# Differential attention beside a recurrent mixer: position term and softmax factors as TensorE products, and each head's output split into four parts

## The reference, cut to what matters

```python
def diff_attention(q, k, v, lam, slopes):      # q, k: 4 heads, 2 maps each of 64 channels; v: 128 channels a head
    ...
    dist = (qpos[:, None] - kpos[None, :])
    s = jnp.einsum('bhcqd,bhckd->bhcqk', qblk, kh) * scale
    s = s - slopes[None, :, None, None, None] * dist
    s = jnp.where(dist >= 0, s, NEG_INF)
    pr = jax.nn.softmax(s, axis=-1)
    attn = pr[:, :, 0] - lam * pr[:, :, 1]
    return jnp.einsum('bhqk,bhkv->bhqv', attn, vh)
```

## Time and profile before

| | |
|---|---|
| median of 3 runs | 1692.66 us (1690.74 to 1696.22) |
| the profiled execution: its own time | 1689.58 us |
| the profiled execution: span | 1687.8 us |
| TensorE busy | 1525.4 us (90% of the span) |
| VectorE busy | 1093.8 us (65%) |
| ScalarE busy | 705.6 us (42%) |
| mean granted clock of TensorE | 0.957 of full speed |

### The profile page before, as it was taken

The page is one execution under the profiler, slowest core; times in us unless marked ns, Lnnn a source line. Parts: engine busy times, 40 slices in busy tenths (PEclk is TensorE's granted clock), DMA queues, the critical chain, the costliest instruction groups (busy, mean ns, idle before and its releaser), DMA issues.

```text
span 1687.8 us, 26133 instructions
## 1 busy us (share of the span) xinstructions
PE 1525.4 (90%) x10702; PEld 1272.3 (75%) x10702; DVE 1093.8 (65%) x1661; ACT 705.6 (42%) x1057; POOL 58.9 (3%) x52
## 2 busy tenths in 40 slices
PE   5999888988989999999989989999999888778892
PEld 4889666866768888888868778787799666777882
DVE  5831766676479737737679997454765446567775
ACT  5422434433444333333444222334344346357773
POOL 0000000000000000000000000000000000222221
PEclk9999889998989999999989999999999999689996
DMA  6220000002412222222312222232243203569896
GB/s 245 100 100 1 2 2 3 3 2 75 151 53 97 101 100 100 100 89 90 122 50 100 100 75 100 77 135 88 88 150 128 72 26 122 192 222 364 322 329 219
DMA packets 37828, 189.69 MB, mean 112 GB/s; under 512 B 4304, under 2 KB 4432, under 8 KB 24400
## 3 DMA queue, kind: packets, MB, share of 16 engines
q1 hardware_dynamic: 30672, 167.08, 28.2%
q0 software_dynamic: 4864, 16.78, 2.7%
q10 hardware_dynamic: 2176, 4.19, 0.7%
HBM read 175.46 MB, written 12.58 MB: 111 GB/s over the span
## 4 chain that ended last, share of the span: by engine, by line
PE 70%; DVE 17%; DMA 6%; ACT 4%; issue 3%; POOL 0%; DVEq 0%; SPq 0%; POOLq 0%; ACTq 0%
PE acc L470 18%; PE acc L472 18%; PE acc L471 18%; DMA raw<-wstream 4%; DVE CA L2382 3%; PE acc L712 2%; DVE wl L1915 2%; PE mb L712 1%; PE mb L614 1%; DVE wl L1903 1%; PE mb L545 1%; PE acc L1015 1%; ACT wh L1230 1%; PE mb L470 1%; PE mb L472 1%
## 5 line engine op out<-in xcount | busy, mean ns | idle before, releaser
L470 PE MATMUL acc<-XH,wh 128*128 128x512 f32 x1008 | 397.3, 394 | 5.9 <-DVE wl L1915 4.9
L472 PE MATMUL acc<-XH,wl 128*128 128x512 f32 x1008 | 393.1, 390 | 0.0
L471 PE MATMUL acc<-XL,wh 128*128 128x512 f32 x1008 | 392.8, 390 | 0.0
L1230 ACT ACTIVATE wh<-raw 128x2048 fp32r<-128x2048 f32 x99 | 189.4, 1915 | 248.2 <-DMA raw<-wstream 248.2
L1915 DVE TENSOR_TENSOR wl<-raw,wh 128x2048 fp32r<-128x2048 f32 x99 | 226.0, 2287 | 71.7 <-ACT wh L1230 68.5
L470 PEld LDWEIGHTS acc<-XH,wh 128*128 128x128 f32 x1008 | 189.7, 188 | 48.1 <-DVE wl L1915 5.8
L471 PEld LDWEIGHTS acc<-XL,wh 128*128 128x128 f32 x1008 | 189.7, 188 | 41.1 <-issue 2.2
L472 PEld LDWEIGHTS acc<-XH,wl 128*128 128x128 f32 x1008 | 189.5, 188 | 39.9
L1251 ACT ACTIVATE ev<-acc 128x512 f32<-128x512 f32 x146 | 85.7, 598 | 217.8 <-PE acc L472 197.1
L1903 DVE TENSOR_TENSOR wl<-raw,wh 128x1024 fp32r<-128x1024 f32 x96 | 117.0, 1223 | 47.2 <-ACT wh L1217 40.9
L1217 ACT ACTIVATE wh<-raw 128x1024 fp32r<-128x1024 f32 x96 | 101.4, 1060 | 35.9 <-DMA raw<-wstream 35.3
(11 more groups left out here) (524 smaller groups left out, 2739.9 us busy)
## 6 DMA issues: line engine op xcount, KB each, us to landing
raw<-wstream SPq DMA_DIRECT2D x99, 1024.0 KB
raw<-wstream SPq DMA_DIRECT2D x96, 512.0 KB
YG<-YT ACTq DMA_DIRECT2D x8, 512.0 KB
XT<-xT SPq DMA_DIRECT2D x2, 1024.0 KB, 9.6
XT<-xT SPq DMA_DIRECT2D x1, 2048.0 KB, 7.8
XD<-HN SPq DMA_DIRECT2D x4, 512.0 KB, 2.6
out<-XTK SPq DMA_DIRECT2D x4, 512.0 KB, 2.6
cst<-consts SPq DMA_DIRECT2D x1, 1230.0 KB, 18.3
```

The costliest lines, as they stand in the source:

```text
L470: mm(out_, a[0], b[0], start=start, stop=False)
L471: mm(out_, a[0], b[1], start=False, stop=False)
L472: return mm(out_, a[1], b[0], start=False, stop=stop)
L1230: actv(wh[:, n % RING].rearrange("p a b c -> p (a b c)"), raw[:, n % RING, :], ACT.Copy).then_inc(hi_done, 1)
```

## The change

The distance table is copied once to float32r (`far`), and a 128x128 diagonal matrix holds the head's slope (`slopes`). `scores` adds, behind the product of each map, a float32r product of `slopes` with `far` over the same w columns, into the same bank. VectorE's `att_scaled` is gone; the maximum (`att_max`) and `exp` read the scores in PSUM. `exp` of a head's first unit waits for the maxima of its first two units.

`att_weights` no longer passes over `SC`: it writes two diagonal matrices `inv` with 1/den and lam/den. `turn` takes a float32 product of each block of each map with them, two for each block where one transpose stood; they add up in PSUM.

The output of heads 0 to 2 is issued in parts: the first product at `s6`, the second at `s7`, the third and fourth in the next pair's `nr`, behind its first products. The head's square, sums and root move to the next pair's `ak`, and `head_spread` to the end of `ak`. Head 3 keeps its old places.

Some names move to other beats: `max1` into level 2 before the level's last VectorE step, `scores2`'s maximum to the end of level 5, `turn2` between the two halves of `gh`, `exps` ahead of `exp3`, the table load behind `exp3`, `hats` to `s4`, `hat_r` ahead of `weights3`, and `weights3` to `s5` just before `turn3`.

```diff
-SIDE = {"l1": ["scores0", "scores1"], "l2": ["max1"], "l3": ["weights1"], "l4": ["scores2"], "x": ["weights2"],
-        "wu": ["turn2", "turned2"], "s2": ["up", "max3"], "s3": ["decay", "up_gate", "exp3", "exps"],
-        "s4": ["weights3", "scaled"], "s5": ["turn3", "turned3", "hats", "hat_r"], "s6": ["out", "square", "hat"],
-        "s7": ["sums", "more"], "y": ["root"], "mu": ["ends"]}
+SIDE = {"l1": ["scores0", "scores1"], "l3": ["weights1"], "l4": ["scores2"], "x": ["weights2"],
+        "wu": ["turned2"], "s2": ["up", "max3"], "s3": ["decay", "up_gate", "exps", "exp3", "root_table"],
+        "s4": ["scaled", "hats"], "s5": ["hat_r", "weights3", "turn3", "turned3"], "s6": ["out", "square", "hat"],
+        "s7": ["out_2nd", "sums", "more"], "y": ["root"], "mu": ["ends"]}
...
 scores(u)
                 for c in range(2):
-                    last = mm(score_of(u, c), QT[64 * c:64 * c + 64, h, i * P:(i + 1) * P],
-                              KD[64 * c:64 * c + 64, h, 0:w], start=True, stop=True)
+                    mm(score_of(u, c), QT[64 * c:64 * c + 64, h, i * P:(i + 1) * P],
+                       KD[64 * c:64 * c + 64, h, 0:w], start=True, stop=False)
+                    last = mm(score_of(u, c), slopes[:, :], far[:, S - w:S], start=False, stop=True)
...
 turn(u)
                 for j in range(u % TT + 1):
-                    last = nc.tensor.transpose(turned_of(u)[:, j * P:(j + 1) * P], SC[:, u % 2, 0, j * P:(j + 1) * P], ident)
+                    for c in range(2):
+                        last = mm(turned_of(u)[:, j * P:(j + 1) * P], SC[:, u % 2, c, j * P:(j + 1) * P],
+                                  inv[:, u % 2, c, :], start=(c == 0), stop=(c == 1))
...
-            def head_out(h):
+            def out_part(h, js):
                 pe.wait_ge(s["at_te"], TT * (h + 1))
-                for j in range(TT):
+                for j in js:
...
+            def head_out(h):
+                out_part(h, (0,) if h < 3 else range(TT))
+            def head_out_2nd(h):
+                if h < 3:
+                    out_part(h, (1,))
...
 nr(ct), behind its first products
                 if ct:
-                    head_spread(ct - 1)
+                    out_part(ct - 1, (2, 3))
 ak(ct)
                 if ct:
                     mu(ct - 1)
+                    head_sums(ct - 1)
...
                     products(hh, 1, KH).then_inc(s["rk_ak"], 1)
+                if ct:
+                    head_spread(ct - 1)
 gh(ct)
                     last.then_inc(s["rk_gh"], 1)
+                    if hh == 0:
+                        turn(TT * ct + 2)
...
 exp(u)
-                act.wait_ge(s["at_mx"], u + 1)
+                act.wait_ge(s["at_mx"], u + 1 + (u % TT == 0))
+                if u >= 2:
+                    act.wait_ge(s["at_t"], u - 1)
...
-                    last = actv(SC[:, u % 2, c, 0:w], SC[:, u % 2, c, 0:w], ACT.Exp, bias=nmx[:, x:x + 1],
+                    last = actv(SC[:, u % 2, c, 0:w], score_of(u, c), ACT.Exp, bias=nmx[:, x:x + 1],
...
 before_mu(ct) on ScalarE
                 if ct:
+                    head_square(ct - 1)
                     mu(ct - 1)
+                    head_root(ct - 1)
...
 att_weights(u)
-                link(v.tensor_scalar(a, a, rden[:, x:x + 1], None, ALU.mult))
-                v.scalar_tensor_tensor(out=a, in0=b, scalar=rden[:, x + 1:x + 2], in1=a, op0=ALU.mult,
-                                       op1=ALU.add).then_inc(s["at_p"], 1)
+                for c in range(2):
+                    last = v.tensor_scalar(inv[:, u % 2, c, :], ident, rden[:, x + c:x + c + 1], None, ALU.mult)
+                last.then_inc(s["at_p"], 1)
...
 head_norm(h)
+                if h < 3:
+                    slopes_of(h + 1)
...
 ak(ct) on VectorE
                     masked(AKRK, hh, 1)
+                if ct:
+                    head_root(ct - 1)
 level(l) on VectorE
                     if l == 2:
                         key_root(ct + 1)
                         att_max(TT * ct)
-                    if l == 5:
-                        att_scaled(TT * ct + 2)
+                        att_max(TT * ct + 1)
...
                     if l == 5:
-                        att_top(TT * ct + 2)
+                        att_max(TT * ct + 2)
...
+            v.tensor_copy(far[:, :], cs("alibi"))
+            slopes_of(0)
             dve.wait_ge(acc_ready, 20)
```

More of the change, by code:

```diff
@@ L187, in build @@
         Fo = at("Fo", [KT, S], ar + 32 * KB)
+        far = at("far", [S], top_of["cst"] + 4 * CO["alibi"][0], F32R)
+        slopes = at("slopes", [P], ar + 56 * KB, F32R)
+        inv = at("inv", [2, 2, P], ar + 56 * KB + 512)
         HH = at("HH", [KT, S], ar, F32R)
@@ L875, in _ @@
             main |= {f"l{l}": level(l) for l in range(1, LEVELS)} | {f"s{c}": enter(c) for c in range(2, NCH)}
-            in_beats(main, {"scores": scores, "turn": turn, "head_out": head_out, "head_sums": head_sums,
+            in_beats(main, {"scores": scores, "turn": turn, "head_out": head_out, "head_out_2nd": head_out_2nd, "head_sums": last_sums,
                             "up": up, "up_gate": up_gate})
@@ L1470, in affine, with root_table, last_square, last_root @@
                      scale=pr("ln_x_w", ct)).then_inc(s["rk_sd"], 1)
+            def root_table(ct):
+                actv(sml[:, 60:61], cs("eps", 0, 1), ACT.Sqrt)
+            def last_square(h):
+                if h == 3:
+                    head_square(h)
+            def last_root(h):
+                if h == 3:
+                    head_root(h)
             def before_mu(ct):
@@ L1969, in _, with att_max, slopes_of @@
             lowered[0] = B0["out"] + 3
-            def att_scaled(u):
-                h, i = divmod(u, TT)
-                w = (i + 1) * P
-                slope = 2.0 ** (-8.0 * (h + 1) / 4)
+            def att_max(u):
+                i = u % TT
+                w, first = (i + 1) * P, P * (i == 1)
                 dve.wait_ge(s["at_sc"], u + 1 + (i == 0))
                 if u >= 2:
-                    dve.wait_ge(s["at_t"], u - 1)
-                for c in range(2):
-                    link(v.scalar_tensor_tensor(out=SC[:, u % 2, c, 0:w], in0=cs("alibi", S - w, S), scalar=slope,
-                                                in1=score_of(u, c), op0=ALU.mult, op1=ALU.add))
-            def att_top(u):
-                w = (u % TT + 1) * P
+                    dve.wait_ge(s["at_e"], u - 1)
                 x = slice(2 * (u % 2), 2 * (u % 2) + 2)
-                link(v.tensor_reduce(mx[:, x], SC[:, u % 2, :, 0:w], AX.X, ALU.max))
+                link(v.tensor_reduce(mx[:, x], mb[:, 2:4, first:first + w], AX.X, ALU.max))
                 v.tensor_scalar(nmx[:, x], mx[:, x], -1.0, None, ALU.mult).then_inc(s["at_mx"], 1)
-            def att_max(u):
-                att_scaled(u)
-                att_top(u)
+            def slopes_of(h):
+                return v.tensor_scalar(slopes[:, :], ident, 2.0 ** (-8.0 * (h + 1) / 4), None, ALU.mult)
             def att_weights(u):
-                w, x = (u % TT + 1) * P, 2 * (u % 2)
-                a, b = SC[:, u % 2, 0, 0:w], SC[:, u % 2, 1, 0:w]
+                x = 2 * (u % 2)
                 dve.wait_ge(s["at_e"], u + 1)
@@ L2251, in _ @@
             main |= {f"l{l}": level(l) for l in range(1, LEVELS)} | {f"s{c}": enter(c) for c in range(2, NCH)}
-            in_beats(main, {"max": att_max, "weights": att_weights, "head_root": head_root,
-                            "decay": decay, "hat_r": hat_r, "scaled": scaled, "hats": hats, "hat": hat, "ends": last_in, "more": more_in})
+            in_beats(main, {"max": att_max, "weights": att_weights, "head_root": last_root, "decay": decay, "hat_r": hat_r, "scaled": scaled, "hats": hats, "hat": hat, "ends": last_in, "more": more_in})
             dve.wait_ge(s["rk_vs"], 7)
```

12 lines of the change are left out of this document (8 added, 4 removed).

## The result

The changed kernel takes 1742.8 us (median of four runs, 1738.0 to 1749.0) against 1691.7 for the kernel before beside it: a ratio of 1.030, 95% interval 1.026 to 1.034. It is 51 us slower. The forecast had the sign, but 20 of the 51 us, and its range ended at 1720. The profiled execution took 1749.0 us, with a span of 1747.2; it is the longest of the four, while the one of the kernel before (1689.6) is short among its own.

A forecast was written before the change was run, and what follows sets the result against it. TensorE bounds a round's front, a chain of hand-overs its tail. Front of round 0 2.35, rounds 1 to 3 13.05, tails 2.4, round 3's tail 2.8: +20.6 on 1689.6, plus 1.8, gives 1712 us; range 1688 to 1720.

The forecast's parts named there:

- step 1: Whole stage: VectorE loses some 15 us of L1979 and some 6 of the weights, costed at nothing in a round's front.
- step 2: Scores: the position product parts the two maps' products, +0.8, +0.8 and +1.1 us by unit, +2.7 a round.
- step 4: Start of rounds 1 to 3: `head_spread` waits for the reciprocal behind VectorE's second mask, level 1 starts +2.0 us later.
- step 3: Turns as products: units 0 and 1 +0.75, unit 2 1.45, unit 3 1.9 us at full clock, 3.5 at half.
- Step 5: Tail of rounds 0 to 2: unit 3's turn late behind `hat_r`, at half clock, `y` +0.8 us, bounds -1.1 and +2.1.
- Rival A: Scores: the position product slips between the maps' products without parting them, 1.55 us a round less, 1706; chance 0.14.
- the forecast's first lines: Tail of a round: L614, square and sums ahead of `y`, 6.3 us a round, are what can come off the path.
- Step 6: Round 3's tail: splits ahead of `weights3` delay unit 3's turn, output ends 2.8 us later; bounds +0.9 and +4.6.
- Rival C: Tails: half the clock lasts longer, +2.1 us in rounds 0 to 2 and +4.6 in the last, 1718; chance 0.10.
- Rival B: Tails: the clock holds at 2.4 GHz, -1.1 us in rounds 0 to 2 and +0.9 in the last, 1704; chance 0.12.

The follow-up runs named there:

- experiment 16: Changed kernel with only ScalarE's and VectorE's lists behind the third state put back in their old order: 1.0160 of the kernel before.
- experiment 4: Changed kernel with transposes and VectorE's position term back, leaving the new places and the new list order: 1.0074 of the kernel before.
- experiment 9: Kernel before plus one product nobody reads behind the fourth and one behind the fifth state of each round: 0.9930 of the kernel before.
- experiment 10: Changed kernel plus filling products, one behind the fourth state and three behind the fifth: 1.0224 of the kernel before.
- experiment 18: Changed kernel with two edits, the maps side by side and the two lists in their old order, no filling products: 1.0011 of the kernel before.
- experiment 6: Changed kernel with both maps' score products issued first, then both position products: 1.0145 of the kernel before.

## Why the prediction was right in sign and short in size

**Right.** VectorE's relief showed nowhere in the front, where TensorE is the cover: it is busy for 49.65 of 51.10 us there (step 1). The pairs are parted (step 2). `head_spread` waits for the reciprocal behind both masks (step 4): 0.88 us, and the stretch up to the scores came to +2.1 in round 2 for a forecast of +2.0. Unit 3's turn waits for `hat_r` and runs 16 records at half the clock (steps 3 and 5): 3.80 us, where 3.5 stood.

**Step 2 is the one that failed.** "By columns, units 0 and 1 go from 0.86 to 1.64, unit 2 from 0.85 to 1.64: +0.8 each time", +1.1 for unit 3, +2.7 a round. Measured in round 2: +4.1, +1.55 and +1.9. Round 2 is the dearest; over the four rounds it is 26.9 us for a forecast of 10.8, so 16 of the 31 us by which the forecast's 20.6 fall short of the table's 51.5. One term was left out and one condition was off.
- The columns were priced rightly, and the change from one shape of product to another was put at nothing. A shape is what the timeline prints as rows*columns: the maps are 64*128, the position products 128*128, the recurrent part 64*64. At 0.43 a record and 0.22 a position product unit 3 comes to 2.16; it took 2.95. The missing 0.8 is 0.2 for each of the four stretches of one shape (map, position, map, position), about 0.1 at either end. Timeline of PE, kernel before, two records on 128 rows between 64*64 products:

```profile
326.56 0.68 PE L712 MATMUL mb<-Qm,TTm 64*64 64x64 f32 x16
327.17 1.12 PE L668 MATMUL acc<-Wr,cst 128*128 128x512 f32 x2
328.23 1.15 PE L712 MATMUL mb<-Vtok,AKRK 64*64 64x64 f32 x32
```

  They cost 1.06, as a map does, and not the 0.86 that I took from L853, which follows a product of its own shape (L628). The same 0.2 stands in the earlier trace rows: the pair costs 1.06, and both maps share it. In the order of the change nothing is shared.
- Units 0 and 1 were costed at the full clock. In round 2 they ran at half of it for most of their 5 us, and so did the first three groups of level 2. But the left-out term alone is larger. In round 0 of experiment 16 the clock is full throughout, and they took 3.22 us: 1.6 by columns, and 1.6 for eight stretches.

```profile
186.61 0.49 PE L602 MATMUL mb<-KD,QT 64*128 64x128 f32 x2
...
189.52 0.38 PE L604 MATMUL mb<-far,slopes 128*128 128x256 f32 x1
```

The other 15 us of the shortfall: 7 between the scores of units 0 and 1 and those of unit 2 (for the most part half the clock in level 2), 3 up to level 1, and some 4 behind unit 2's scores.

**Rival A did not come.** Nothing slips past the product between the maps. The Trainium skill (TensorE: Matmul & The Clock Gate, Part 3, The mechanism) says that matmuls start and end in program order and only weight loads are pulled ahead; the trace agrees, with the second map starting 1.48 us behind the first in unit 3.

**Step 5 left out what it could have won.** It forecast "+0.8" for a tail with a turn 2.4 us late, half the clock and a split output (its own end times, 356.8 and 356.1, give 0.7), and for its stretch, unit 3's scores to `y`, that meant +0.95; round 2 has +2.0, of which 0.8 is step 2's error again. So it fitted. But I treated the order of the lists as a price set off against the split output. Experiment 16 shows it as the dearest single line of the change after the pairs: without it the new tail is 2.5 us shorter than before, so the late weights and the clock they lose cost 4.4 us a round there. Part of the 2.5 us is the clock, since the kernel before is as short with it held (16.5). But the 16.4 of experiment 16 hold 1.9 us more of scores and the longer turn, so the split output does shrink the tail, as the forecast's first lines say, and the list hid it.

**Step 4 was short in the sum**: +9.3 for +6.0 over three rounds. Round 2 fitted (+2.5); rounds 1 and 3 have half the clock from 254.3 and 401.0 us, just behind the wait, as in experiment 4. **Step 6** said +2.8 for round 3's tail with the head whole; from unit 3's scores to `y` it came to +3.4.

**The clock.** Rival C asked for longer half-clock stretches in the tail; they came in the front. The lower level lasts 38.3 us in the stage of the kernel before and 73.8 in that of the changed one. If TensorE had been the limit in all of the 35 us more, they would have cost half of that, 18 of the 52 us (an estimate from these two sums, and an upper bound). Experiments 9 and 10 show that this clock is not fixed by the stage: filled gaps bring it back, to 12.6 and 40.0 us at the lower level. Rival B's rule, that a transpose does not count as work for the clock as a product does (the Trainium skill, TensorE: Matmul & The Clock Gate, Part 4), is not decided. In the changed kernel the turn by products ran at half the clock all the same. In experiment 16 it did not; but there the wait ahead of it had gone too, and experiment 9 kept the clock with transposes and filling products.

What stays open: how far below the kernel before the kernel of experiment 18 would come with filling products of the right size, and what TensorE does in the 0.2 us of a change of shape. Neither was tried.

## What to carry to other kernels

Before an instruction is put between two that run side by side, count how often TensorE will change its shape, and price each stretch from a row with the same neighbours: here the order of four instructions was worth 26 of the 40 us that the position products cost. When work moves off one engine, look at what stands in front of the hand-over that is left on its list; one product late is a wait, and a wait can lose the clock for what follows. The kernel before, with two products a round that nobody reads, takes 0.7% less than without them, and no kernel with the new products comes as low: here it was cheaper to keep TensorE's clock through a chain of waits than to shorten the chain, as long as the filling was shorter than the wait.

## What the hardware showed that I had not expected

- A change of shape has a price of its own. A float32 record of 512 columns is followed by the next of its shape after 0.43 us; behind a product of another shape it is 0.53, in front of one 0.52. That holds for 128 rows between 64*64 products (L668) as for the 64 rows of a map, and at 128 columns too (0.21 behind another shape, 0.11 within; L628). Groups of 64*64 products lose about half of it at their start.
- A float32r product of 512 columns takes 0.42 us alone between 64-row products, two in a row take 0.34 and 0.32 (experiment 6), and in a long run each takes 0.22. So a stretch costs 0.2 us besides its columns, whether it holds one product or two; at 128 columns and the full clock one takes 0.26 and two 0.37, with the same 0.2. The Trainium skill (TensorEngine Tiling (Array Packing), Key Properties) says that a change of the tiling mode drains TensorE; that is in line with a fixed price for each change, and no run here shows what happens inside it.
- The granted clock fell inside stretches in which TensorE was busy without a gap by its records: 6.80 us busy of 6.80, at 0.50. Before it fell the engine had waited 0.88 us for the reciprocal, run level 1 and 1.95 us of small sums (L558). A busy share of 100% in a window is no promise of the upper clock in it.
- 0.8 us of filling in each of two gaps a round took the time at the lower level in the stage from 38.3 to 12.6 us (experiment 9).
